# The seven-product scheme starts one chunk earlier in the two SwiGLU up projections behind an RMS norm

## The chip, the core and the metric

The kernel runs on one core of a Trainium2 chip. The metric is device time in microseconds (us), the median of several executions. Five engines share the work: PE (TensorE) multiplies, DVE (VectorE) and ACT (ScalarE) do elementwise work, SP (SyncE) issues the big loads, and POOL (GpSimd) a few small ones. Each engine runs its own instructions in order and waits on semaphores that others raise.

## The reference, cut to what matters

Two blocks run one after the other on 256 tokens of width 1024. The change lies in the first block, which has two layers; each layer has a SwiGLU in front of its mixer and another behind it:

```python
for l in range(DEPTH):                                   # DEPTH = 2
    mod = (cs @ ada_w[l] + ada_b[l]).reshape(...)
    h = _rmsnorm(x, norm_g[l, 0]) * (1.0 + mod[:, 0, 1]) + mod[:, 0, 0]
    x = x + 0.5 * mod[:, 0, 2] * _swiglu(h, ffn_w_gate[l, 0], ffn_w_up[l, 0], ffn_w_down[l, 0])
    ...                                                  # norm, mixer, norm
    x = x + 0.5 * mod[:, 2, 2] * _swiglu(h, ffn_w_gate[l, 1], ffn_w_up[l, 1], ffn_w_down[l, 1])

def _swiglu(h, w_gate, w_up, w_down):
    return (jax.nn.silu(h @ w_gate) * (h @ w_up)) @ w_down   # 1024 -> 2816 -> 1024
```

All of it is float32.

## The kernel before

Tokens are the moving side: `h` is held as 8 tiles of 128 features x 256 tokens. Weights stream from DRAM through `ring`, a buffer of three slots; SP starts a load as soon as the slot's last user is done (`chunk_done`). An up projection (stage `up0` in front of the mixer, `up2` behind it) is 11 chunks of 2 MB, each with 4 groups of 128 outputs (two gate tiles, two up tiles). Between them lie chunks of the modulation weights ("ada"), which DVE multiplies and sums with `ada_sums` (four instructions of line 1792). The string `order` sets the sequence: six ada chunks in `up0`, four in `up2`. Both stages run in both layers, so four times in all.

A chunk goes one of three ways:

- **Chunk 0, the head** (line 778). PE multiplies the not yet normalised `raw`. After its first group PE also sums the squares. DVE takes the reciprocal root (2053), takes out that group (`raw_out`, 1812 and 1813), writes the eight normalised tiles of `h` (`normalise`, line 2071), and ACT adds the shift to each (1493) and raises `h`. Then DVE takes out the other three groups; 1844 joins an up tile with its gate tile when ACT has done the silu.
- **A plain chunk** (line 791). 32 products of 128x128 weights with 256 tokens. PE runs a float32 product as two instructions, so that is 64 in the profile.
- **A chunk with seven products** (`fast_chunk`, line 710): the Strassen-Winograd scheme on 2x2 blocks. It has 7 products of 8 matmuls on 128 tokens, 112 instructions. I call them P1 to P7. DVE must first make sums of the weights (`weight_sums`, lines 1871 to 1876, four instructions of 1024 columns) and, once a stage, of the tokens (`token_sums`, lines 1883 to 1888). P2 needs the first token sum. ACT copies partial results out (`parts_out`), and DVE adds them up (`quadrants`, from line 1909), multiplies gate and up (`gate_up`, 1922) and makes sums for the down projection (`mid_sums`).

A seven-product chunk uses three banks of PSUM in turn: `TRIOS = ((0, 1, 2), (3, 4, 5), (6, 7, 2))`, counted from the first such chunk (`lin.fast`). P1, P3, P5 and P7 use the first bank of a trio, P2 and P6 the second, P4 the third. Bank 2 stands in two neighbouring trios, since 6, 7, 2 is followed by 0, 1, 2. It comes free with the first instruction of `quadrants`, which DVE runs after the weight sums of the next chunk.

Before the change `lin.fast` is 2: chunk 0 is the head, chunk 1 is plain, chunks 2 to 10 use seven products.

Of the kernel before, what the change touches and what calls it, by code (L numbers as in the profile page):

```python
# [15 lines left out]
P = 128  # L16
# [3 lines left out]
DT = D // P  # L20
# [164 lines left out]
def stages():  # L185


    up_rms = lambda src, order: Linear(11, 4, 32 * P, src, order.count("a"), 1, order, 2, biased=2,
                                       token_sums=4, silu=9, mid=9, mid_sums=10)
    down = lambda src: Linear(4, 2, 44 * P, src)  # L190
    down_fast = lambda src: Linear(4, 2, 44 * P, src, fast=0, x_tile=DT)
    norm = with_(uses(b5=1), raw=DT, squares=DT, most_squares=1, root=1, scaled=DT, h=DT)
    ln = with_(uses(b5=1, b6=1), mean=DT, squares=DT, root=1, h=DT)
    ln_fused = with_(ln, most_x=1, scaled=DT)
    logits = with_(uses(b4=2, b5=2, b6=2, b7=2), probs=HG, bias_in=16)
    mix = uses(b0=2, b1=2, b2=2, b3=2)
    prologue = {
        "load_x": with_(uses(b0=1, b1=1, b2=1, b3=1), cond_in=16, cond_set=1, x_tile=DT),
        "bias_rows": uses(b4=1),
        "ada0": Linear(0, 4, 32 * P, "none", adas=4),  # L200
    }
    layer = {
        "norm0": norm, "up0": up_rms("up", "mmmamamamamamamm" "m"), "down0": down_fast("down"),
        "norm1": norm,
        "qk": Linear(6, 4, 32 * P, "w_qk", 6, 1, biased=4), "v": Linear(3, 4, 32 * P, "w_v"),
        "logits0": logits,
        "ccch": Linear(4, 4, 32 * P, "w_ccch"),
        "logits1": logits,
        "cb": Linear(2, 4, 32 * P, "w_cb"),
        "logits2": with_(logits, maxima=1),  # L210
        "gate_a": Linear(2, 4, 32 * P, "w_gates", 2), "mix0": mix,
        "gate_b": Linear(2, 4, 32 * P, "w_gates", gate_c=1), "mix1": mix,
        "weigh": with_(uses(b4=1), weighted=1), "mix2": with_(mix, **uses(b6=1, b7=1)),
        "conv_out": Linear(2, 4, 32 * P, "w_conv_out"),
        "combine": with_(uses(b4=1, b5=1), shares=2, mixed=MIX),
        "attn_out": Linear(1, 8, 32 * P, "w_attn_out", merged=DT),
        "wo": Linear(2, 4, 32 * P, "w_o"), "cond": {"cond_in": 16, "cond_set": 1},
        "norm2": norm, "up2": up_rms("up", "mmmamammammammm"), "down2": down_fast("down"),
    }
    second = {  # L220
        "final_norm": with_(norm, scaled=0, h=0),
        "mod3": {"h": DT},
        "xm": Linear(4, 4, 32 * P, "m_xm", 4, 1, biased=4), "z": Linear(4, 4, 32 * P, "m_z", 2, order="mmamma"),
        "mconv": {"conv": MT, "xc": 1},
        "q": Linear(1, 16, 16 * P, "m_q"), "k": Linear(1, 16, 16 * P, "m_k"),
        "vT": Linear(1, 16, 16 * P, "m_v"),
        "gates": with_(uses(b4=1), gate_rows=1, gate_size=1, gate_logs=1, rows=1),
        "vtok": Linear(1, 8, 16 * P, "m_v_again"),
        "rows_t": with_(uses(b4=1, b5=1, b6=1), floor=1, decays=1),
        "scores": uses(b0=1, b1=1, b2=1, b3=1),  # L230
        "numer": with_(uses(b0=2, b1=2, b2=2, b3=2, b7=1), mvar=MH, mroot=MH, mscale=MH),
        "h_t": with_(uses(b4=2, b5=2, b6=2, b7=2), mh=MT),
        "m_out": Linear(4, 2, 32 * P, "m_out", 3, order="mamamam"), "ln0": ln_fused,
        "up3": Linear(11, 4, 32 * P, "up_3", 11, order="ma" * 11, fast=1, token_sums=4, silu=10, mid=10), "down3": down("down_3"),
        "s5_b": {"s5_dt": 1, "s5_turns": 1, "s5_trig": 1, "s5_lags": 1, "s5_consts": 1, "s5_tables": 1, "s5_waves": 1},
        "ln1": with_(ln, most_x=1),
        "s5_v": Made(3),
        "s5_k": uses(b4=1, b7=1),
        "s5": with_(uses(b0=2, b4=1, b5=1, b6=1, b7=1), free2=2, us_act=11, us_dve=21, states=4, gelu=4, gelu_raw=1, gelu_moved=1),
        "glu": Linear(4, 4, 32 * P, "glu"), "ln2": with_(ln_fused, x_last=1),  # L240
        "router": with_(uses(b4=3, b5=1), top=1, ratio=1, gate=1, picked=1),
        "tokens": uses(b0=1, b1=1, b2=1, b3=1),
    }
    expert = {
        "gather": with_(uses(b4=2, b5=2, b6=2, b7=3), picked=1),
        "upE": Rounds(4, (4, 4, 3), DT, "up_e"), "downE": Sides((0, 8, 15, 22), "down_e"),
        "scatter": uses(b4=2, b5=2, b6=2, b7=2),
    }
    epilogue = {"ln3": with_(ln, scaled=DT), "store": uses(b0=1, b1=1, b2=1, b3=1)}
    return [(prologue, 1), (layer, DEPTH), (second, 1), (expert, NE), (epilogue, 1)]  # L250
# [131 lines left out]
def build(nc, dram, out, periods):  # L382
    plan = Plan()
    with ExitStack() as ctx:
# [9 lines left out]
        h = sb("h_t", [P, DT, S])  # L394
# [32 lines left out]
        mid, act2 = tiles(0, FT), tiles(FT, 2)  # L427
# [52 lines left out]
        def two_columns(a, pairs):  # L480
# [78 lines left out]
        signal = {k: sem(k.replace(" ", "_")) for k in sorted(plan.total)  # L559
                  if k != "chunk" and not k.startswith("of ")}  # L560
        bank_free = [signal[f"free{b}"] for b in range(BANKS)]
# [25 lines left out]
        def reads(p, b, k=0, i=0, per=0):  # L587


            return p.of(f"free{b}", k + 1, i, per)  # L590
# [98 lines left out]
        def _(pe):  # L689
# [154 lines left out]
                    idle_products(p, 13)  # L844

            def ffn(up, down, area, ready=None, after=None, rms_of=None):
                linear(up, lambda k, n: h[:, k, :], ready, rms_of=rms_of,
                       fast=(area, lambda k, t: lambda i: h[:, 4 * k + i, half_of_tokens[t]],
                             lambda k: (signal["token_sums"], up.of("token_sums", k))))
                pe.wait_ge(signal["mid"], up.of("mid", up.what.fasts))  # L850

                linear(down, lambda k, n: mid[:, k, :], after=after,
                       fast=(downs, lambda k, t: lambda i: mid[:, 2 * i + k, half_of_tokens[t]],
                             lambda k: (signal["mid_sums"], up.of("mid_sums", up.what.also["mid_sums"]))))
# [75 lines left out]
            p = place("load_x")  # L930
# [10 lines left out]
            p = place("bias_rows")  # L941
# [34 lines left out]
            p = place("gates")  # L976
# [4 lines left out]
            for pair in range(3 * MT // 2):  # L981
# [3 lines left out]
                for part in range(2):  # L985
                    k = 2 * pair + part
                    src = (mq, mk, mvt)[k // MT][:, k % MT, :]
# [7 lines left out]
            p = place("vtok")  # L995
# [778 lines left out]
        def _(dve):  # L1774
# [140 lines left out]
            def gated_fast(p, buf, dst, np, area, sums=None, normalise=None, down=None):  # L1915

                lin = p.what

                def gate_up(j):
                    n, both = j - lin.fast, area.both(j % 2)  # L1920
                    dve.wait_ge(signal["silu"], p.of("silu", n + 1))
                    dve.tensor_tensor(dst[:, 2 * j:2 * j + 2, :], both[:, 0], both[:, 1], ALU.mult).then_inc(signal["mid"], 1)  # L1922
                    if down:
                        dve.wait_ge(signal["mid"], p.of("mid", n + 1))
                        mid_sums(j)

                done = {n: p.slot(pos) for pos, (kind, n) in enumerate(lin.order) if kind == "main"}
                for pos, (kind, j) in enumerate(lin.order):
                    where = p.slot(pos)
                    if kind == "ada":  # L1930
                        sums(j, 0, where)
                    elif j < lin.fast - 1:
                        gated_chunk(p, buf, dst, j, 0, where, normalise)
                    elif j == lin.fast - 1:
                        token_sums(p, np, area)
                    else:
                        weight_sums(p, j, where, area, done[j - 2] if j > lin.fast + 1 else None)
                        if j == lin.fast:
                            gated_chunk(p, buf, dst, j - 1, 0, done[j - 1])
                            if down:  # L1940
                                dve.wait_ge(bank_free[3], reads(p, 3, lin.at[j - 1][3][2]) + 1)
                                mid_sums(0, lin.fast)
                        else:
                            if j > lin.fast + 1:
                                gate_up(j - 2)
                            quadrants(p, j - 1, area)
                last = lin.chunks - 1
                if down:
                    weight_sums(down, 0, down.slot(0), downs, done[last - 1])
                gate_up(last - 1)  # L1950
                quadrants(p, last, area)
                gate_up(last)
# [714 lines left out]
            p = sp5  # L2667
# [397 lines left out]
```

## Time and profile before

| | us |
|---|---|
| median of 3 runs (3187.36 to 3188.55) | 3187.43 |
| the profiled execution | 3183.68 |
| its span, first to last instruction | 3181.5 |
| PE busy | 3024.8 (95%) |
| DVE busy | 1431.4 (45%) |
| ACT busy | 562.6 (18%) |

Busy time says how full an engine is over the whole program. Which of them holds the end is read from the chain of waits that ended last, and inside a stage from the timeline, where each row gives the start, the duration, and in brackets how long the engine sat idle just before and what it waited for. The four up stages lie at 46 to 191 us, 634 to 775, 851 to 995 and 1440 to 1581. The mean granted clock of TensorE is 0.987 of full speed.

### The profile page before, as it was taken

The page shows a single profiled execution, that of the slowest core. Times are in us where ns is not written, and L with a number is a line of the kernel's source. Part 1 is how long each engine was busy: PE and PEld are TensorE (multiplying, and loading weights), DVE is VectorE, ACT ScalarE, POOL GpSimd, SP SyncE. Part 2 cuts the span into 40 slices and gives each one's busy share as a digit, 9 for nine tenths or more (in the row PEclk, how much of TensorE's full clock was granted, in tenths as well). Part 3 has the DMA queues.
Part 4 walks back from the last instruction along what each step waited for, and adds up shares of the span by engine and source line. Part 5 has one row for each costly group of instructions (what it writes and reads, how often), then busy time and mean ns, then how long its engine had stood idle before and what let it go on. Part 6 is the DMA issues. An engine that isn't in the chain of part 4 may idle for free.

```text
span 3181.5 us, 64710 instructions
## 1 busy us (share of the span) xinstructions
PE 3024.8 (95%) x27390; PEld 2635.5 (83%) x27391; DVE 1431.4 (45%) x2829; ACT 562.6 (18%) x1326; POOL 15.6 (0%) x27
## 2 busy tenths in 40 slices
PE   5999999999999999999999999996999999999999
PEld 4998888899999888889998778985787678767875
DVE  6863333277486423336755448898321112111212
ACT  1111004121111100312111302135211101110111
POOL 0000000000000000000000000000000000000000
PEclk8999999999999999999999999998999999999999
DMA  7746645355375564535637346822287898889885
GB/s 304 309 181 224 239 159 192 129 209 229 138 291 204 200 259 159 192 133 212 242 134 277 133 160 265 322 116 81 102 322 284 307 357 330 317 312 359 321 310 205
DMA packets 55527, 732.94 MB, mean 230 GB/s; under 512 B 6609, under 2 KB 6793, under 8 KB 10805
## 3 DMA queue, kind: packets, MB, share of 16 engines
q1 hardware_dynamic: 51364, 716.68, 58.7%
q0 software_dynamic: 3984, 13.74, 1.2%
q8 instruction: 129, 2.11, 0.3%
q14 instruction: 50, 0.40, 0.0%
HBM read 729.31 MB, written 4.23 MB: 231 GB/s over the span
## 4 chain that ended last, share of the span: by engine, by line
PE 79%; DMA 12%; DVE 6%; issue 2%; ACT 1%; SPq 0%; DVEq 0%; ACTq 0%
PE psum L791 25%; PE psum L710 22%; PE psum L1265 11%; PE psum L1308 10%; DMA ring<-in_up_dram 4%; PE psum L778 3%; DMA ring<-in_up_e_dram 3%; PE psum L865 3%; DVE ring L1792 2%; DMA ring<-in_w_qk_dram 1%; DMA ring<-in_down_e_dram 1%; PE psum L1289 1%; PE psum L1324 1%; DVE work L1778 1%; DMA ring<-in_ada_dram 1%
## 5 line engine op out<-in xcount | busy, mean ns | idle before, releaser
L791 PE MATMUL psum<-h_t,ring 128*128 128x256 f32 x2944 | 642.8, 380 | 8.2 <-DMA ring<-in_w_qk_dram 5.2
L791 PEld LDWEIGHTS psum<-h_t,ring 128*128 128x128 f32 x2944 | 558.0, 190 | 90.5 <-issue 11.5
L1265 PE MATMUL psum<-h_t,ring 128*64 128x96 f32 x11264 | 470.3, 246 | 10.0 <-DMA ring<-in_up_e_dram 9.7
L1265 PEld LDWEIGHTS psum<-h_t,ring 128*64 128x64 f32 x11264 | 466.5, 137 | 13.0 <-issue 11.9
L710 PE MATMUL psum<-work,ring 128*128 128x128 f32 x2880 | 344.5, 276 | 8.6 <-DVE work L1922 8.6
L710 PEld LDWEIGHTS psum<-work,ring 128*128 128x128 f32 x2880 | 333.5, 193 | 9.3 <-issue 9.3
L1308 PE MATMUL psum<-ring,work 128*96 128x512 f32 x704 | 304.1, 593 | 1.2 <-DMA ring<-in_down_e_dram 1.0
L1792 DVE SCALAR_TENSOR_TENSOR ring<-ring,cond 128x1024 f32<-128x1024 f32 x240 | 279.3, 1220 | 57.3 <-DMA ring<-in_ada_dram 57.3
L710 PE MATMUL psum<-work 128*128 128x128 f32 x2528 | 296.7, 276 | 4.2 <-DVE work L1876 4.2
L791 PE MATMUL psum<-work,ring 128*128 128x256 f32 x1344 | 294.9, 382 | 4.2 <-DVE work L1922 2.6
L710 PEld LDWEIGHTS psum<-work 128*128 128x128 f32 x2528 | 290.2, 193 | 4.3 <-DVE work L1876 4.3
L791 PEld LDWEIGHTS psum<-work,ring 128*128 128x128 f32 x1344 | 256.5, 191 | 41.2 <-DVE work L1922 2.7
L1308 PEld LDWEIGHTS psum<-ring,work 128*96 128x96 f32 x704 | 114.1, 163 | 185.5 <-issue 183.1
L2829 DVE TENSOR_TENSOR work<-work,psum 128x256 f32 x176 | 74.1, 421 | 401.1 <-PE psum L1265 401.1
L710 PE MATMUL psum<-h_t,ring 128*128 128x128 f32 x1472 | 181.6, 277 | 14.0 <-DMA ring<-in_up_dram 10.3
L710 PEld LDWEIGHTS psum<-h_t,ring 128*128 128x128 f32 x1472 | 172.0, 192 | 18.3 <-issue 8.6
L2835 DVE COPY work<-psum 128x512 f32<-128x512 f32 x16 | 11.1, 691 | 283.6 <-PE psum L1308 283.6
L778 PE MATMUL psum<-work,ring 128*128 128x257 f32 x448 | 101.8, 385 | 30.2 <-DVE work L2042 26.5
L778 PEld LDWEIGHTS psum<-work,ring 128*128 128x128 f32 x448 | 85.7, 192 | 44.3 <-issue 31.6
L1763 ACT ACTIVATE work<-psum 128x512 f32<-128x512 f32 x16 | 9.6, 597 | 541.7 <-PE psum L1308 541.7
L1871 DVE TENSOR_TENSOR work<-ring 128x1024 f32<-128x1024 f32 (+1 forms) x62 | 82.2, 1326 | 49.6 <-DMA ring<-in_up_dram 49.4
L710 PE MATMUL psum<-h_t,work 128*128 128x128 f32 x736 | 89.7, 275 | 0.0
(375 smaller groups left out, 2449.6 us busy)
## 6 DMA issues: line engine op xcount, KB each, us to landing
ring<-in_up_e_dram SPq DMA_DIRECT2D x64, 2048.0 KB, 7.8
ring<-in_ada_dram SPq DMA_DIRECT2D x60, 2048.0 KB, 7.9
ring<-in_up_dram SPq DMA_DIRECT2D x55, 2048.0 KB, 12.0
ring<-in_down_e_dram SPq DMA_DIRECT2D x32, 1792.0 KB, 8.6
ring<-in_down_dram SPq DMA_DIRECT2D x20, 2816.0 KB, 10.0
ring<-in_up_e_dram SPq DMA_DIRECT2D x32, 1536.0 KB, 8.5
ring<-in_down_e_dram SPq DMA_DIRECT2D x16, 2048.0 KB, 8.3
ring<-in_w_qk_dram SPq DMA_DIRECT2D x12, 2048.0 KB, 9.7
```

The costliest lines, as they stand in the source:

```text
L710: mm = pe.matmul(bank(bank_of)[:, pair * P:(pair + 1) * P], w, right(i), start=(first and pair == 0 and i == 0), stop=(pair == lin.pairs - ...
L778: mm = pe.matmul(psum[:, b * 512:b * 512 + S + 1], ring[:, slot, (m * DT + k) * P:(m * DT + k + 1) * P], raw[:, k, :], start=(k == 0), sto ...
L791: mm = pe.matmul(half(b), w, moving(k, j * lin.groups + m), start=(k == 0), stop=(k == depth - 1))
L865: mm = pe.matmul(half(b), h[:, k, t * P:(t + 1) * P], ring[:, slot, k * 512 + n * S:k * 512 + (n + 1) * S], start=(k == 0), stop=(k == DT ...
L1265: mm = pe.matmul(half(b)[lo:hi, 0:width], w[:, lo:hi], h[:, k, 0:width], start=(k == 0), stop=(k == lin.depth - 1))
L1289: mm = pe.matmul(half(b)[:, 0:width], h_tok[:, t, f * P:(f + 1) * P], sel[:, t, 0:width], start=(t == 0), stop=(t == TT - 1))
L1308: mm = pe.matmul(bank(2 * side + n)[0:slots(n), :], mid[:, k, n * P:n * P + slots(n)], ring[:, slot, (k - first) * 512:(k - first + 1) * 512],
L1324: mm = pe.matmul(half(b), y_pos[0:slots(n), n, f * P:(f + 1) * P], gate_sel[0:slots(n), n, :], start=(n == 0), stop=(n == lists - 1))
L1778: dve.tensor_tensor(o, a, b, op).then_inc(dve_done, steps.one())
L1792: e = dve.scalar_tensor_tensor(w, w, 1.0, cond[:, :], ALU.mult, ALU.mult, accum_out=col)
L1871: dve.tensor_tensor(s1, a21, a22, ALU.add).then_inc(signal["weight_sums"], 1)
L2829: dve.tensor_tensor(o, o, half(b), ALU.mult).then_inc(bank_free[b], 1)
```

## The change

`fast` becomes 1, so chunk 1 uses seven products too, and the trios are counted from it: chunk 4 now has banks 0, 1, 2, where it had 6, 7, 2. PE waits for all of `h` in front of chunk 1. On DVE the order around the head changes.

```diff
-    up_rms = lambda src, order: Linear(11, 4, 32 * P, src, order.count("a"), 1, order, 2, biased=2,
-                                       token_sums=4, silu=9, mid=9, mid_sums=10)
+    up_rms = lambda src, order: Linear(11, 4, 32 * P, src, order.count("a"), 1, order, 1, biased=2,
+                                       token_sums=4, silu=10, mid=10, mid_sums=11)
...
+                all_h = lambda: pe.wait_ge(signal["h"], ready.of("h", DT)) if up.what.head else None
...
+                    elif j == 0 and lin.head:
+                        def normalise_first():
+                            normalise()
+                            weight_sums(p, 1, done[1], area)
+
+                        gated_chunk(p, buf, dst, 0, 0, where, normalise_first)
+                        token_sums(p, np, area)
+                        if down:
+                            dve.wait_ge(bank_free[3], reads(p, 3, lin.at[0][3][2]) + 1)
+                            mid_sums(0, 1)
...
-                        weight_sums(p, j, where, area, done[j - 2] if j > lin.fast + 1 else None)
+                        if j > 1 or not lin.head:
+                            weight_sums(p, j, where, area, done[j - 2] if j > lin.fast + 1 else None)
+                        if j == lin.fast and lin.head:
+                            continue
```

On DVE, at the head of `up0`, the rows before run from the normalised tiles straight to the head's second, third and fourth group:

```order
L2071 SCALAR_TENSOR_TENSOR h_t<-x_t,gain,rms 128x256 x8
L1811 ISA
L1812 COPY small<-psum 128x1 [waits full1]
L1813 TENSOR_TENSOR work<-psum,rms 128x256
L1842 REGISTER_ALU
L1843 ISA [waits dve_done]
L1844 SCALAR_TENSOR_TENSOR work<-work,small 128x256 [waits biased]
L1812 COPY small<-psum 128x1 [waits full2]
```

At the same place of the changed kernel, whose lines are numbered up to 14 higher there:

```order
L2085 SCALAR_TENSOR_TENSOR h_t<-x_t,gain,rms 128x256 x8
L1871 ISA
L1872 TENSOR_TENSOR work<-ring 128x1024 [waits chunk_in2]
L1873 TENSOR_TENSOR ring<-ring 128x2x512
L1874 ISA
L1875 TENSOR_TENSOR work<-work,ring 128x1024 [waits weight_sums]
L1876 REGISTER_ALU
L1877 TENSOR_TENSOR work<-ring,work 128x1024 [waits weight_sums]
L1812 ISA
L1813 COPY small<-psum 128x1 [waits full1]
L1814 TENSOR_TENSOR work<-psum,rms 128x256
```

The four weight sums of chunk 1 (`ring` is the weight buffer, `work` holds the sums) now stand between the normalised tiles and the second group of the head; the token sums still come behind the head's fourth group.

On PE, chunk 1 of `up0` before:

```order
L773 REGISTER_ALU [waits chunk_in2]
L791 MATMUL psum<-h_t,ring 128x256 [waits h,free0]
L791 MATMUL psum<-h_t,ring 128x256 [waits h] x7
L791 MATMUL psum<-h_t,ring 128x256 [waits free1]
L791 MATMUL psum<-h_t,ring 128x256 x7
```

On PE, chunk 1 of `up0` now:

```order
L730 REGISTER_ALU [waits chunk_in2]
L710 MATMUL psum<-h_t,ring 128x128 [waits h,free0]
L710 MATMUL psum<-h_t,ring 128x128 x7
L727 ISA
L738 ISA [waits free1,weight_sums]
L710 MATMUL psum<-work 128x128 [waits token_sums]
L710 MATMUL psum<-work 128x128 x7
```

The second product, on the sums in `work`, waits for bank 1, which the head's second group frees on DVE, and for the first token sum.

On PE, chunk 4 of `up0` before:

```order
L730 ISA [waits chunk_in1]
L710 MATMUL psum<-h_t,ring 128x128 [waits free6]
L710 MATMUL psum<-h_t,ring 128x128 x7
L727 REGISTER_ALU
L710 MATMUL psum<-work 128x128 [waits free7,weight_sums]
```

On PE, chunk 4 of `up0` now:

```order
L730 REGISTER_ALU [waits chunk_in1]
L710 MATMUL psum<-h_t,ring 128x128 [waits free0]
L710 MATMUL psum<-h_t,ring 128x128 x7
L727 REGISTER_ALU
L710 MATMUL psum<-work 128x128 [waits free1,weight_sums]
```

Chunk 4 moved from the trio 6, 7, 2 to 0, 1, 2. Its fourth product uses bank 2 in both kernels; the user of bank 2 before it was chunk 2, and is now chunk 3.

## Rows read from the trace of the kernel before

**Rows 1.** The page: busy time; shares of the chain that ended last.
```profile
PE 3024.8 (95%) x27390; PEld 2635.5 (83%) x27391; DVE 1431.4 (45%) x2829; ACT 562.6 (18%) x1326; POOL 15.6 (0%) x27
PE 79%; DMA 12%; DVE 6%; issue 2%; ACT 1%; SPq 0%; DVEq 0%; ACTq 0%
```

**Rows 2.** The chain in order of time, first `up0`: start, us, what.
```profile
56.90 13.81 PE psum L791 x64
70.71 12.52 PE psum L710 x112
```

**Rows 3.** Timeline, head of the first `up0`: start, us, engine, line, operation.
```profile
52.86 0.15 DVE L1812 COPY small<-psum 128x1 f32<-128x1 f32 x1
...
56.74 13.97 PE L791 MATMUL psum<-h_t,ring 128*128 128x256 f32 x64
...
60.48 1.22 DVE L1871 TENSOR_TENSOR work<-ring 128x1024 f32<-128x1024 f32 x1
...
65.15 0.41 DVE L1852 TENSOR_TENSOR work<-work,psum 128x256 f32<-128x256 f32 x1
```

**Rows 4.** Timeline, head of the second `up0`.
```profile
858.32 0.15 DVE L1812 COPY small<-psum 128x1 f32<-128x1 f32 x1
...
860.83 0.48 DVE L1844 SCALAR_TENSOR_TENSOR work<-work,small 128x256 f32<-128x256 f32 x1 [2.03 <-ACT work L1451]
...
861.11 13.97 PE L791 MATMUL psum<-h_t,ring 128*128 128x256 f32 x64
861.23 0.15 DVE L1812 COPY small<-psum 128x1 f32<-128x1 f32 x1
...
861.63 0.15 DVE L1812 COPY small<-psum 128x1 f32<-128x1 f32 x1
...
862.29 0.49 DVE L1844 SCALAR_TENSOR_TENSOR work<-work,small 128x256 f32<-128x256 f32 x1 [0.18 <-ACT work L1451]
862.69 0.68 DVE L1883 TENSOR_TENSOR work<-h_t 128x512 f32<-128x512 f32 x1
```

**Rows 5.** Timeline, head of the second `up2`.
```profile
1446.73 0.15 DVE L1812 COPY small<-psum 128x1 f32<-128x1 f32 x1
...
1450.61 13.97 PE L791 MATMUL psum<-h_t,ring 128*128 128x256 f32 x64
```

**Rows 6.** Timeline, chunk 4 of the second `up2`, with the issue of its load.
```profile
1477.98 12.12 SPq L643 DMA_DIRECT2D ring<-in_up_dram  x2
...
1490.70 1.22 DVE L1871 TENSOR_TENSOR work<-ring 128x1024 f32<-128x1024 f32 x1 [0.92 <-DMA ring<-in_up_dram]
...
1490.80 2.05 PE L710 MATMUL psum<-h_t,ring 128*128 128x128 f32 x16 [1.20 <-DMA ring<-in_up_dram]
...
1496.25 1.95 PE L710 MATMUL psum<-h_t,ring 128*128 128x128 f32 x16
...
1497.03 0.41 DVE L1909 TENSOR_TENSOR work<-work,psum 128x256 f32<-128x256 f32 x1
```

**Rows 7.** Timeline, first `up0`: waits of PE in chunks 5 and 8.
```profile
115.23 0.41 DVE L1909 TENSOR_TENSOR work<-work,psum 128x256 f32<-128x256 f32 x1
...
115.70 2.05 PE L710 MATMUL psum<-h_t,ring 128*128 128x128 f32 x16 [0.56 <-DVE work L1909]
...
156.06 2.05 PE L710 MATMUL psum<-h_t,ring 128*128 128x128 f32 x16 [1.08 <-DVE work L1909]
```

**Rows 8.** Timeline of PE: first matmuls behind longer idle times, in four stages.
```profile
190.64 2.72 PE L710 MATMUL psum<-work,ring 128*128 128x128 f32 x22 [2.15 <-DVE work L1922]
...
995.18 4.35 PE L710 MATMUL psum<-work,ring 128*128 128x128 f32 x22 [2.15 <-DVE work L1922]
...
1938.34 5.26 PE L710 MATMUL psum<-work 128*128 128x128 f32 x32 [4.18 <-DVE work L1876]
...
2072.11 28.11 PE L791 MATMUL psum<-work,ring 128*128 128x256 f32 x129 [2.55 <-DVE work L1922]
```

**Rows 9.** Busy time by stretch: stretch, length, PE, PEld, DVE, ACT, POOL, then PEclk.
```profile
996.50:998.00 1.50, 1.50 (x9) 1.50 (x9) 1.41 (x5) 0.00 (x0) 0.00 (x0) 0.50 0.91 390
```

## What the change should do to the time

> **What bounds the kernel now.** I read the page first: PE is busy for 95% of the span, and 79% of the chain that ended last is PE [rows 1]. Time that PE gains or loses inside an up stage therefore reaches the end, unless a load or DVE holds PE up at the next step anyway. So I followed the chain through the stages, and then read the timeline of each up stage row by row: the head, chunk 1, and each later place where PE sat idle. The four up stages repeat each other almost to the hundredth; where one row stands for several stages I say for how many.
>
> Two things are to be seen. A plain chunk costs PE 13.81 us and a seven-product chunk 12.52 us, so 1.79 us for each of the seven products [rows 2]. And chunk 1 is the place where DVE has the most to do in a row, while chunk 4 is where PE waits for a load in all four stages (1.20 to 1.35 us).
>
> **Part 1, the products.** Chunk 1 falls from 13.81 to 12.52 us on PE [rows 2]: -1.29 us, four times, -5.2 us. This is on the path, since PE goes on without a gap from the head to chunk 1 and on to chunk 2.
>
> **Part 2, a new wait for the token sum.** P1 of chunk 1 needs only `h`, which is complete before the head ends. P2 needs the first token sum and bank 1, and DVE now reaches both late, because it does the weight sums first. Step by step for the first `up0`, counted from the start of the second group's copy, at 52.86 us, when DVE is done with normalising [rows 3]:
> - The four weight sums take 65.15 - 60.48 = 4.67 us [rows 3]. Chunk 1 landed long before, so they don't wait.
> - The second group, from its copy to the third group's copy: from copy to join 862.29 - 861.63 = 0.66, and from join to the next step 861.23 - 860.83 = 0.40, together 1.06 us; ACT's silu has long been done by then.
> - From the third group's copy to the token sums: 862.69 - 861.23 = 1.46 us [rows 4].
> - The first token sum 0.68 us [rows 4], and 0.06 us until PE sees it (in rows 7, DVE's instruction of 0.41 us started at 115.23, and PE at 115.70).
>
> The sum is 7.93 us, so the token sum is there at 60.79. The head leaves PE free at 56.74 [rows 3], and P2 could start after P1, at 58.53. The wait is 2.26 us. A product behind a wait shows 2.05 instead of 1.95 us [rows 6], so 0.10 more: 2.36 us. Both `up2` have the same offset: in the second one 1450.61 - 1446.73 = 3.88 us [rows 5] against 56.74 - 52.86 = 3.88, and in the first 3.89. In the second `up0` DVE normalises later: the offset is 861.11 - 858.32 = 2.79 us [rows 4], and the wait grows to 7.93 - 2.79 - 1.79 = 3.35, with the restart 3.45 us. Together 3 x 2.36 + 3.45 = +10.5 us.
>
> So chunk 1 gets longer: by 1.07 us three times and by 2.16 us once. The later products don't wait: P3 needs the third token sum signal, 1.2 us after the first, while P2 takes 1.79 us. The weight sums of chunk 2 follow on DVE at about 64 us, before PE needs them. Weight sums no longer run during chunk 2's first steps, and `quadrants`, `gate_up` and `mid_sums` of chunk 1 come in; DVE waits there for loads anyway, so I cost them at nothing. Without that cover they would cost up to 2 us a stage.
>
> **Part 3, the banks.** Chunk 4 now follows chunk 3 on bank 2. In the second `up2` chunk 4 lands at 1490.7: DVE starts its weight sums and PE its P1 together. DVE reaches the first instruction of `quadrants` (chunk 3) at 1497.03 and ends it at 1497.44, while P4 of chunk 4 started at 1496.25 [rows 6]. In the changed kernel P4 must wait for that instruction: 1.19 + 0.06 + 0.10 = 1.35 us. The first `up2` has the same rows with 1.18. Both together: +2.7 us. The load doesn't come earlier to help, as it is issued when PE ends chunk 2 (1477.98) [rows 6], and PE ends that later. Chunks 7 and 10 meet the same pair of banks, but in `up2` DVE is there in time (its step at 1530.41, P4 at 1533.77).
>
> In both `up0` such waits exist already, in chunks 5 and 8, with 0.56 and 1.08 us [rows 7]; they go, and chunks 4 and 7 get them, up to 1.35 each. There an ada chunk stands beside every chunk, and loads set the pace between waits (0.48 us in chunk 6) [rows 7]: two chunks later a wait in the one comes off the load wait of the other or adds to it. Following the loads through, the new waits put chunk 8 behind by 1.4 us, and chunk 8's own old wait makes up for it. I take 0 for both stages; the bounds are -1.8 us each (old waits gone, new ones hidden) and +1.1 each (both new ones at 1.35, against 1.64 gone).
>
> **Part 4, the clock.** After an idle time of PE the granted clock can be at the lower of its two levels, 1.2 instead of 2.4 GHz. Of four waits of 2.15 us at the hand-over to the down projection, one was followed by slow matmuls: 4.35 us for the same 22 instructions that took 2.72 elsewhere [rows 8], at a granted clock of 0.50 [rows 9]. That cost 1.63 us. A wait of 2.55 us left the clock alone, one of 4.18 us didn't: 32 matmuls took 5.26 us [rows 8], where 32 take 3.74 at full clock. The new waits are 2.3 us (three) and 3.4 us (one). By these rows the short ones fall rarely and the long one lies between 2.55 and 4.18; I take one fall, +1.6 us, and 0 to 4 as bounds (0 to +6.5 us).
>
> The Trainium skill, "TensorE: Matmul & The Clock Gate", Part 1, says that the monitor which sets the clock runs freely and doesn't start with the kernel, so that the same kernel shows other numbers of slow matmuls from run to run. The trace agrees in that four equal waits of 2.15 us had one fall. By that rule the number of falls is a matter of position, and the sum has no fixed last term.
>
> **The sum.** -5.2 + 10.5 + 2.7 + 0 + 1.6 = +9.6 us. Against the profiled execution of 3183.68 us that is 3193.3; that execution was 3.75 us below the median of the runs shown, so the median goes from 3187.43 to **3197.0 us**. 0.2% of this kernel is 6.4 us, about what a measurement can tell from no change.
>
> **The rivals.**
> - **Most new waits meet the lower clock** (three or four falls). For it: the waits stand one behind each norm, where nothing else keeps PE busy, and all are longer than the 2.15 us that fell once. Against it: one of four, and 2.55 without. Three falls give 8.0 + 4.9 = 12.9, four 14.5 us: 3200.3 to 3202.
> - **The loads swallow the late chunk 1** (not slower). PE waits 1.2 to 1.35 us for the load of chunk 4 in all four stages, so a chunk 1 that is 1.07 us late would cost nothing if that load kept its time. Part 2 would then be worth only 2.16 - 1.3 = 0.9, and the whole 0.9 + 2.7 = +3.6 us: 3191.0, within the bound. It decides wherever the load of chunk 4 is issued by something other than PE's end of chunk 2. Against it: the load is issued within 1 us of that end [rows 6].
> - **The token sums come in time** (faster, but within the bound): if DVE reached them before P1 ends, part 2 would be 0 and the clock untouched, -5.2 + 2.7 = -2.5 us: 3184.9. It decides if the offset of 2.8 to 3.9 us were 6 or more. Against it: rows 3 to 5.
> - **No wait for bank 2** in `up2`, and the old ones in `up0` gone: -5.2 + 10.5 - 3.6 = +1.7 us, 3189.1.
>
> That the change doesn't do what it says can be left out: the order on PE and DVE shows it.
>
> **How the numbers follow.** My forecast with 0 to 2 falls has a chance of 0.72 (3195.4 to 3198.7 by the terms, 3193 to 3201 with the bounds of part 3); three or four falls 0.12; loads swallow it 0.06; no wait for bank 2 0.05; token sums in time 0.05. The range leaves out the not-slower rivals and the top of the first one: 3193.0 to 3201.0. Slower by over 0.2% (above 3193.8): the forecast less a small part at its lower end, and the first rival: 0.83. Within: the other three and that part, 0.14. Faster by over 0.2% would need the token sums in time and the bank waits gone: 0.03.
>
> **What would show it.** In each up stage of the changed kernel, PE should sit idle in chunk 1 before P2 for 2.2 to 2.3 us (3.3 in the second `up0`), released by DVE's first token sum, and in chunk 4 before P4 for about 1.25 us, released by `quadrants`. Chunk 1 should take 14.9 us (16.0). The matmuls behind the chunk 1 wait tell the falls: 16 instructions take 1.95 at full clock. I am wrong if P2 waits under 1.3 us, if chunk 4's load wait is gone, or if the old waits of `up0` stay.

## The result, and the profile after

| | before | after |
|---|---|---|
| median, us | 3187.43 | 3201.11 |
| the profiled execution, us | 3183.68 | 3202.76 |
| its span, us | 3181.5 | 3200.7 |
| mean granted clock | 0.987 | 0.983 |

The changed kernel is slower: 13.7 us by the medians, a ratio of 1.0041 with an interval of 1.0027 to 1.0056. Timed again beside other runs of before it was 1.0045 (1.0030 to 1.0061). All medians below are of the fast executions; one slow execution each of the last two kernels (3850 and 10672 us) is left out.

The page after, busy time and the shares of the chain that ended last, against [rows 1]. PE has 192 instructions more (four chunks of 112 for four of 64), and DVE holds 8% of the chain instead of 6%:

```profile
PE 3033.6 (95%) x27582; PEld 2648.4 (83%) x27583; DVE 1456.0 (45%) x2869; ACT 569.5 (18%) x1342; POOL 15.6 (0%) x27
PE 77%; DMA 11%; DVE 8%; issue 3%; ACT 1%; SPq 0%; DVEq 0%; ACTq 0%
```

Where it went shows in the busy time by stretch. Each row runs from the head's second group to the start of the down projection, one row for each up stage in order; the columns are those of [rows 9], and the third number from the end is the clock. Before:

```profile
46.30:190.64 144.34, 138.38 (x1122) 134.24 (x1120) 112.00 (x187) 28.82 (x68) 0.00 (x0) 1.00 0.68 267
634.48:775.17 140.69, 137.23 (x1122) 133.86 (x1120) 102.54 (x171) 28.81 (x68) 0.00 (x0) 1.00 0.60 232
850.67:995.18 144.51, 138.28 (x1121) 134.15 (x1120) 111.99 (x188) 28.84 (x68) 0.00 (x0) 1.00 0.64 247
1440.17:1580.76 140.59, 137.24 (x1122) 133.86 (x1120) 102.54 (x171) 28.82 (x68) 0.00 (x0) 1.00 0.60 231
```

After:

```profile
46.52:196.05 149.53, 140.24 (x1169) 137.76 (x1168) 118.03 (x197) 30.41 (x72) 0.00 (x0) 0.98 0.66 257
641.80:785.08 143.28, 136.43 (x1170) 134.35 (x1168) 108.51 (x181) 30.42 (x72) 0.00 (x0) 1.00 0.59 227
860.32:1009.69 149.37, 139.10 (x1170) 136.28 (x1168) 118.27 (x198) 30.42 (x72) 0.00 (x0) 0.99 0.62 241
1455.06:1599.98 144.92, 138.05 (x1169) 135.97 (x1168) 108.50 (x181) 30.41 (x72) 0.00 (x0) 0.99 0.58 224
```

The four stages are longer by 5.19, 2.59, 4.86 and 4.33 us, 17.0 together. The second shows the clock at 1.00; in the fourth it is 0.99, in the third 0.99 and in the first 0.98.

The timeline of PE in chunk 1 after. P1 and P2 of the first `up0`, then P2 of the other three stages:

```profile
56.97 1.95 PE L710 MATMUL psum<-h_t,ring 128*128 128x128 f32 x16
60.97 5.47 PE L710 MATMUL psum<-work 128*128 128x128 f32 x32 [2.06 <-DVE work L1884]
...
656.32 3.81 PE L710 MATMUL psum<-work 128*128 128x128 f32 x32 [2.13 <-DVE work L1884]
...
876.28 5.46 PE L710 MATMUL psum<-work 128*128 128x128 f32 x32 [3.58 <-DVE work L1884]
...
1469.58 5.44 PE L710 MATMUL psum<-work 128*128 128x128 f32 x32 [2.14 <-DVE work L1884]
```

P2 waits for DVE's first token sum (line 1884) in all four stages. The 32 matmuls of P2 and P3 then take 3.81 us once and 5.44 to 5.47 us three times. The granted clock of the first of these stretches is 0.68, so part of it ran at the lower level of 1.2 GHz; that of the second is 1.00 (stretch, length, PE busy, clock):

```profile
60.97:66.24 5.27, 5.27 (x32) 0.68 0.57 243
...
656.32:660.00 3.68, 3.68 (x33) 1.00 0.82 347
```

DVE around it in the first `up0`, which answers to [rows 3]: the first weight sum, the second group's copy, the fourth group's join, the first token sum:

```profile
53.09 1.22 DVE L1872 TENSOR_TENSOR work<-ring 128x1024 f32<-128x1024 f32 x1
...
57.76 0.15 DVE L1813 COPY small<-psum 128x1 f32<-128x1 f32 x1
...
59.83 0.49 DVE L1845 SCALAR_TENSOR_TENSOR work<-work,small 128x256 f32<-128x256 f32 x1 [0.18 <-ACT work L1452]
60.23 0.68 DVE L1884 TENSOR_TENSOR work<-h_t 128x512 f32<-128x512 f32 x1
```

From 53.09 to PE's start at 60.97 it is 7.88 us (the prediction's sum was 7.93).

Chunk 4, P4 behind bank 2, in the first `up0` and the second `up2`, which answers to [rows 6], and a load wait of chunk 6 in the first `up0`:

```profile
106.03 2.05 PE L710 MATMUL psum<-h_t,ring 128*128 128x128 f32 x16 [1.24 <-DVE work L1910]
...
127.89 2.54 PE L710 MATMUL psum<-h_t,ring 128*128 128x128 f32 x16 [1.94 <-DMA ring<-in_up_dram]
130.22 4.91 PE L710 MATMUL psum<-work 128*128 128x128 f32 x32
...
1515.38 2.05 PE L710 MATMUL psum<-h_t,ring 128*128 128x128 f32 x16 [1.08 <-DVE work L1910]
```

And the hand-over to the down projection, which answers to [rows 8]. Before, one of four was slow; after, three of four:

```profile
196.05 3.73 PE L710 MATMUL psum<-work,ring 128*128 128x128 f32 x22 [2.15 <-DVE work L1923]
...
785.08 2.72 PE L710 MATMUL psum<-work,ring 128*128 128x128 f32 x22 [2.15 <-DVE work L1923]
...
1009.69 4.35 PE L710 MATMUL psum<-work,ring 128*128 128x128 f32 x22 [2.15 <-DVE work L1923]
...
1599.98 4.34 PE L710 MATMUL psum<-work,ring 128*128 128x128 f32 x22 [2.15 <-DVE work L1923]
```

### The profile page after: what moved, and what is told of

Its sections match the earlier page's. It is cut to its first block, busy times and chain, and to the rows that moved or that the text cites. A ratio compares the mean times of both kernels' runs of the same rounds, so it can differ in the third digit from the quotient of the medians.

```text
span 3200.7 us, 65252 instructions
## 1 busy us (share of the span) xinstructions
PE 3033.6 (95%) x27582; PEld 2648.4 (83%) x27583; DVE 1456.0 (45%) x2869; ACT 569.5 (18%) x1342; POOL 15.6 (0%) x27
## 4 chain that ended last, share of the span: by engine, by line
PE 77%; DMA 11%; DVE 8%; issue 3%; ACT 1%; SPq 0%; DVEq 0%; ACTq 0%
PE psum L791 24%; PE psum L710 23%; PE psum L1266 11%; PE psum L1309 9%; DMA ring<-in_up_dram 4%; DMA ring<-in_up_e_dram 4%; PE psum L866 3%; PE psum L778 2%; DVE ring L1793 2%; DMA ring<-in_w_qk_dram 1%; PE psum L1290 1%; PE psum L1325 1%; DVE work L1779 1%; DMA ring<-in_w_v_dram 1%; DMA ring<-in_ada_dram 1%
## 5 line engine op out<-in xcount | busy, mean ns | idle before, releaser
L791 PE MATMUL psum<-h_t,ring 128*128 128x256 f32 x2688 | 587.1, 380 | 7.9 <-DMA ring<-in_w_qk_dram 4.9
L791 PEld LDWEIGHTS psum<-h_t,ring 128*128 128x128 f32 x2688 | 509.2, 190 | 84.0 <-issue 11.3
L710 PE MATMUL psum<-work,ring 128*128 128x128 f32 x3008 | 362.8, 277 | 8.6 <-DVE work L1923 8.6
L710 PEld LDWEIGHTS psum<-work,ring 128*128 128x128 f32 x3008 | 351.0, 194 | 9.4 <-issue 9.4
L710 PE MATMUL psum<-work 128*128 128x128 f32 x2656 | 318.9, 280 | 14.1 <-DVE work L1884 9.9
L710 PEld LDWEIGHTS psum<-work 128*128 128x128 f32 x2656 | 311.8, 196 | 15.0 <-DVE work L1884 6.0
L791 PEld LDWEIGHTS psum<-work,ring 128*128 128x128 f32 x1344 | 257.5, 192 | 40.2 <-DVE work L1923 2.2
L710 PE MATMUL psum<-h_t,ring 128*128 128x128 f32 x1600 | 197.7, 277 | 18.5 <-DMA ring<-in_up_dram 12.3
L710 PEld LDWEIGHTS psum<-h_t,ring 128*128 128x128 f32 x1600 | 187.3, 192 | 22.9 <-issue 10.6
L778 PEld LDWEIGHTS psum<-work,ring 128*128 128x128 f32 x448 | 85.7, 192 | 44.1 <-issue 31.4
L710 PE MATMUL psum<-h_t,work 128*128 128x128 f32 x800 | 97.5, 275 | 0.0
```

The lines of the kernel that those rows point to most:

```text
L710: mm = pe.matmul(bank(bank_of)[:, pair * P:(pair + 1) * P], w, right(i), start=(first and pair == 0 and i == 0), stop=(pair == lin.pairs - ...
L778: mm = pe.matmul(psum[:, b * 512:b * 512 + S + 1], ring[:, slot, (m * DT + k) * P:(m * DT + k + 1) * P], raw[:, k, :], start=(k == 0), sto ...
L791: mm = pe.matmul(half(b), w, moving(k, j * lin.groups + m), start=(k == 0), stop=(k == depth - 1))
```

## The experiments

A "fall" below means matmuls behind a wait that run at the lower clock for some us. Its price is mostly 1.6 to 1.7 us: 5.44 to 5.47 instead of 3.81, 4.34 instead of 2.72. "Filled" means that PE runs products in a wait whose results nobody reads. "Stage lengths" are the lengths of the stretches shown above, from the head's second group to the start of the down projection. The diffs are shortened ("...") and the comments in them are mine.

### The changed kernel again

No edit. It is there so that the next three can be set against it on the same chip.

> The changed kernel again, beside the others. Its profiled execution had 16 slow instructions or more (lower granted clock) behind three of the four new waits in chunk 1, each worth about 1.6 us. If these falls are a matter of position, a new execution shows another number of them (0 to 4 in chunk 1), while the waits themselves stay at 2.1 us (three) and 3.6 us (one), and chunk 1 takes 14.9 us where no fall is and 16.5 where one is. If the falls belong to the waits as such, the same three or four are there again. Median against before: +10 to +15 us by both.

Measured: 3203.19 against 3190.00 of before, +13.2 us. The waits are in the same places (2.06, 2.14, 3.10 and 2.14 us before P2), but the falls are not: P2 is slow in the first three stages and not in the last, and of the hand-overs the first two are slow. Two rows of it that were the other way round above, P2 in the first and in the second `up2`:

```profile
655.72 5.44 PE L710 MATMUL psum<-work 128*128 128x128 f32 x32 [2.14 <-DVE work L1884]
...
1470.71 3.81 PE L710 MATMUL psum<-work 128*128 128x128 f32 x32 [2.14 <-DVE work L1884]
```

So the places of the waits belong to the kernel, and the falls to the execution. (The wait of the second `up0` was 3.10 us here and 3.58 above; the other three agree within 0.01.)

### The trios turned: no wait for bank 2 in chunk 4

```diff
-                for b, many in zip(TRIOS[(j - fast) % len(TRIOS)], (3, 2, 1)):
+                for b, many in zip(TRIOS[(j - fast + turn) % len(TRIOS)], (3, 2, 1)):   # turn = 2
```

> Only the turn of the bank trios differs from the changed kernel: the first seven-product chunk takes 6, 7, 2, so that chunks 5 and 8 meet the doubled bank 2 as before the change, and no longer chunk 4. My theory of the banks: the wait of 1.1 to 1.2 us before the fourth product of chunk 4 is gone in all four stages; in both up2 nothing takes its place (-1.35 us each), in both up0 the waits of chunks 5 and 8 come back (0 in sum). The wait before the second product of chunk 1 stays at 2.1 and 3.6 us, since the token sums come as late as before. The time falls by 2.7 us against the changed kernel. Rival, that P2 waits for bank 1 and not for the token sum: with bank 7 in place of bank 1 the wait would fall under 1 us in all four stages, and the time by 6 us or more.

Measured: 3202.53, +12.5 us. P4 of chunk 4 waits in no stage any more. In this trace neither `up2` has a fall inside the stage, and they last

```profile
640.07:782.21 142.14, 136.16 (x1170) 134.28 (x1168) 108.49 (x181) 30.42 (x72) 0.00 (x0) 1.00 0.60 229
...
1452.99:1594.84 141.85, 136.16 (x1170) 134.28 (x1168) 108.47 (x181) 30.42 (x72) 0.00 (x0) 1.00 0.60 229
```

142.14 us where the changed kernel without a fall had 143.28: 1.14 us, the size of the bank wait. In both `up0` the waits of chunks 5 and 8 are back. P2 of chunk 1 waits as before (2.06, 2.14, 3.17, 2.13), so bank 1 is not what it waits for: it is the token sum. The bank term is real in the trace, and too small to show in the median: 2.7 us less than the changed kernel was expected, and 0.7 less was measured.

### Trios turned, and the token sums right behind the weight sums

```diff
+                            token_sums(p, np, area)        # behind weight_sums(p, 1, ...)
...
                         gated_chunk(p, buf, dst, 0, 0, where, normalise_first)
-                        token_sums(p, np, area)
```

> As the kernel with turned trios, and the four token sums stand right behind the weight sums of chunk 1, ahead of the head's second, third and fourth group. If the token sums alone held PE up, PE goes through chunk 1 without a wait in three stages (chunk 1 12.5 us, and 0.8 us more in the second up0), and the time falls by 9 to 11 us against the kernel with turned trios. My theory, that DVE's work behind the norm is too long whatever its order: the second product is in time, but ACT's first copy for chunk 1 now stands behind its silu of the head's third group, which DVE takes out 2.6 us later than now, so the third product waits for that copy: 2.4 us in three stages and 2.6 us behind a wait of 0.8 in the second up0. Time then within 2 us of the kernel with turned trios.

Measured: 3204.93, no gain. P2 now starts without a wait in three stages, and P3 waits instead. In the second `up0` both wait, P2 for 2.25 us (0.8 was expected) and P3 for 1.47. P2 and P3 of the first `up0`:

```profile
58.88 1.95 PE L710 MATMUL psum<-work 128*128 128x128 f32 x16
62.87 2.46 PE L710 MATMUL psum<-work 128*128 128x128 f32 x16 [2.04 <-ACT work L1381]
```

The releaser is ACT's copy of P1 and P2 (line 1381). On ACT it stands behind the second silu of the head, and that waited 6.17 us for DVE to take out the third head group (line 1814), which the token sums have pushed back:

```profile
61.86 0.51 ACT L1452 ACTIVATE work<-work,small 128x256 f32<-128x256 f32 x1 [6.17 <-DVE work L1814]
62.27 0.36 ACT L1381 ACTIVATE work<-psum 128x256 f32<-128x256 f32 x1
```

So moving the token sums alone only moves the 2 us from P2 to P3. That DVE's work is too long "whatever its order", as I expected, does not follow: the interleaved order below does away with the wait.

### The wait before P2 filled with products that nobody reads

```diff
+                if n == 0 and lin.head:
+                    for _ in range(9):                     # between P1 and P2
+                        pe.matmul(bank(7)[:, 0:P], ones[:, :], ones[:, :], start=True, stop=True)
```

> The changed kernel, with nine products of ones by ones (18 instructions, 2.0 us) into the idle bank 7 on PE between the first and the second product of chunk 1; their results are never read. The wait for the token sum is thus filled, but not shortened. If the lower clock behind it comes from PE's idle time, chunk 1 takes 14.9 us in three stages and 16.0 in the second up0, with the second product at full clock, and the time falls by 1.6 us for each fall that the changed kernel has there (three in its profile: 4 to 5 us). If the clock falls for another reason, slow instructions stay in chunk 1 or at its start, and the time stays within 1 us of the changed kernel. If the products get in the way (bank 7, weight loads), chunk 1 gets longer.

Measured: 3195.49, +5.5 us against before (interval of the ratio 1.0005 to 1.0024) and 7.7 us less than the changed kernel on the same chip. Nothing that the kernel needs comes earlier; PE only stays busy. P2 is fast in all four stages, in the second `up0` too, where 1.19 us of the wait are left. The first `up0`, then the second:

```profile
60.97 2.17 PE L737 MATMUL psum<-ones 128*128 128x128 f32 x18
63.20 3.84 PE L710 MATMUL psum<-work 128*128 128x128 f32 x32
...
876.39 3.84 PE L710 MATMUL psum<-work 128*128 128x128 f32 x32 [1.19 <-DVE work L1887]
```

So it is PE's idling that brings the falls in chunk 1. One trace could be chance, but the mean granted clock over all executions agrees: 0.984 for the changed kernel (9), 0.987 with the wait filled (11), 0.987 for before (24). The gain is larger than I can count: eight of the twelve P2 waits in three traces of unfilled kernels were followed by a fall, 2.7 a run, or 4.4 us.

### Seven products in chunk 1 with DVE's order interleaved

On DVE the head now runs: first weight sum, first token sum, two weight sums, head groups two and three, two token sums, fourth weight sum, fourth token sum, head group four. The trios are turned.

```diff
...                                                        # turn = 2 as above
+                            first[0](); tokens[0](); first[1](); first[2]()   # weight sums, token sums
...
+                        def behind(m):                     # behind head group m, counted from 0
+                            if m == 2:
+                                tokens[1](); tokens[2](); first[3](); tokens[3]()
...
-                        token_sums(p, np, area)
```

> The seven products in chunk 1 stay, the trios are turned so that the first such chunk takes banks 6, 7, 2, and DVE's order at the head is interleaved: first weight sum, first token sum, second and third weight sum, head groups two and three, two token sums, fourth weight sum, fourth token sum, head group four. If the 10.5 us of waits are owed to the order on DVE alone (theory), chunk 1 shows no wait in three stages and about 0.65 us in the second up0; then each stage from the start of its head to the start of its down projection is shorter than in the kernel before by 0.8 to 1.3 us (0.6 in the second up0), no clock falls in chunk 1, and the median lies 3 to 5 us below the kernel before (ratio 0.9985 to 0.999). If the loads or ACT's copies give the wait back (rival: as P3 did when only the token sums were moved), a wait of 1.5 to 2 us shows at P3 or later in chunk 1 and the median is 4 to 10 us above the kernel before.

Measured: 3187.54 against 3188.52, ratio 1.0000 (0.9989 to 1.0011). That is between the two expectations. Chunk 1 is as the theory has it: P1 to P3 of the first `up0` without a gap, and the only wait left, before P3 of the second `up0`:

```profile
56.89 1.95 PE L710 MATMUL psum<-h_t,ring 128*128 128x128 f32 x16
58.67 3.74 PE L710 MATMUL psum<-work 128*128 128x128 f32 x32
...
865.86 2.05 PE L710 MATMUL psum<-work 128*128 128x128 f32 x16 [0.53 <-DVE work L1919]
```

The stages tell where the gain went:

```profile
46.45:190.80 144.35, 136.97 (x1170) 134.50 (x1168) 117.62 (x197) 30.42 (x72) 0.00 (x0) 1.00 0.69 267
636.39:775.90 139.51, 135.93 (x1170) 134.20 (x1168) 108.18 (x181) 30.41 (x72) 0.00 (x0) 1.00 0.61 234
851.15:996.20 145.05, 137.40 (x1169) 134.65 (x1168) 117.88 (x198) 30.37 (x72) 0.00 (x0) 1.00 0.64 248
1440.62:1579.83 139.21, 135.93 (x1170) 134.21 (x1168) 108.19 (x181) 30.41 (x72) 0.00 (x0) 1.00 0.61 234
```

Both `up2` are shorter than before by 1.18 and 1.38 us, the 1.29 us of part 1. The first `up0` is as long as before (144.35 and 144.34) and the second longer by 0.54, though PE is busy for 1.41 and 0.88 us less: with an ada chunk beside every chunk, PE waits longer for later loads. The longest load wait of before behind chunk 4 of the first `up0`, in chunk 6, and that of this kernel, in chunk 7:

```profile
123.59 2.05 PE L710 MATMUL psum<-h_t,ring 128*128 128x128 f32 x16 [0.48 <-DMA ring<-in_up_dram]
```

```profile
137.14 2.05 PE L710 MATMUL psum<-h_t,ring 128*128 128x128 f32 x16 [1.39 <-DMA ring<-in_up_dram]
```

Chunk 5 too waits for its load, 1.31 us, where it did not before. So in these traces seven products in chunk 1 pay in `up2` alone, 2.6 us together.

### The same, and the hand-overs filled

```diff
+                if up.what.head:                           # ahead of the wait for mid
+                    b, _, k = up.what.at[up.what.chunks - 2][1]
+                    pe.wait_ge(bank_free[b], reads(up, b, k) + 1)
+                    for _ in range(9):
+                        pe.matmul(bank(b)[:, 0:P], ones[:, :], ones[:, :], start=True, stop=True)
```

> As the kernel with the interleaved order, and PE runs nine products of ones by ones (18 instructions, about 2.2 us) in the wait of 2.15 us in front of each of the four first down projections; their result is never read. If PE's idle time is what lowers the granted clock (theory), the first 22 instructions of all four down projections take 2.7 us and the median falls by another 2 to 5 us (one to three falls of 1.6 us), 5 to 9 us below the kernel before. If the clock falls by its own pace whatever PE does there (rival), the median is that of the interleaved order within 1 us and slow matmuls show elsewhere.

Measured: 3182.02 against 3188.52, ratio 0.9979 (0.9969 to 0.9988), the fastest of all kernels here. All four down projections start at full clock. The fill in the first `up0` and the 22 instructions behind it:

```profile
188.61 2.17 PE L855 MATMUL psum<-ones 128*128 128x128 f32 x18
190.93 2.72 PE L710 MATMUL psum<-work,ring 128*128 128x128 f32 x22
```

The traces account for about as much: the stage lengths add up to 567.36 us against 570.13 before, -2.8, and 17 of the 28 unfilled hand-overs in seven traces were slow, 2.4 a run, 3.9 us. Together 6.7, and 6.5 were measured. The falls as the cause are argued here from that count. The mean granted clock doesn't show them: it is 0.987 over the twelve executions of the interleaved kernel and 0.987 over these twelve. And this trace has a fall that none of the other nine has, at the head of the second `up0`, where the same 16 matmuls took 3.72 us before, behind a wait of 2.04:

```profile
845.76 5.40 PE L778 MATMUL psum<-work,ring 128*128 128x257 f32 x16 [2.03 <-issue]
```

### The kernel before with its hand-overs filled

The same lines in the kernel before.

> The kernel before, with the same nine products of ones by ones in the wait in front of each first down projection. Theory: no fall at these four places, median 2 to 5 us below the kernel before. Rival (the clock falls by its own pace): within 1 us of the kernel before.

Measured: 3186.52 against 3188.52, ratio 0.9996 (0.9987 to 1.0005). This doesn't decide: 3.9 us less lies inside the interval, none as well. No hand-over is slow in its trace, but two load waits of chunk 4 that were 1.30 and 1.35 us before are 2.27 and 2.03 here, and both are followed by a fall. The first:

```profile
687.00 2.62 PE L710 MATMUL psum<-h_t,ring 128*128 128x128 f32 x16 [2.27 <-DMA ring<-in_up_dram]
689.41 4.84 PE L710 MATMUL psum<-work 128*128 128x128 f32 x32
```

Why these loads came later was not tried.

### The changed kernel with both fills

The nine products between P1 and P2, and the nine at the hand-over.

> The changed kernel with both fills: nine products of ones by ones between P1 and P2 of chunk 1 and nine in front of each first down projection. Set against the kernel before with the second fill alone it shows what the change costs when the clock has no place to fall: by terms 1 to 3 of the prediction 8.0 us (theory). If the change costs more than these terms by something other than the clock (rival), the difference is 10 us or more.

Measured: 3193.96; 7.4 us above the kernel before with its hand-overs filled, near the 8.0 of the theory. Its trace has no fall in any up stage or hand-over, so it shows parts 1 to 3 of the prediction by themselves:

```profile
46.60:192.76 146.16, 141.26 (x1206) 138.60 (x1204) 118.14 (x198) 30.39 (x72) 0.00 (x0) 1.00 0.67 262
636.67:779.75 143.08, 140.45 (x1205) 138.37 (x1204) 108.43 (x181) 30.40 (x72) 0.00 (x0) 1.00 0.59 228
855.03:1002.09 147.06, 141.31 (x1206) 138.64 (x1204) 118.21 (x198) 30.38 (x72) 0.00 (x0) 1.00 0.63 244
1445.60:1588.72 143.12, 140.44 (x1205) 138.37 (x1204) 108.45 (x181) 30.37 (x72) 0.00 (x0) 1.00 0.59 228
```

Against the stages of before, which have no fall inside either, that is +1.82, +2.39, +2.55 and +2.53: 9.3 us. (The stages of the kernel before with filled hand-overs are no measure for it, as they hold the two falls at loads.) Against the kernel before without a fill the median is 5.4 us higher, and 9.3 less the 3.9 of the hand-overs is 5.4 too. But the kernel with P2's wait alone filled was 5.5 above the runs of before beside it, so between these two kernels the second fill shows no gain.

## Why the prediction was right, and which term was too small

The direction was right, and so were the mechanisms. The median came out 4.1 us above the forecast and 0.1 us above the end of the range. (The range's lower end was tighter than its own terms: 3195.4 less twice the bound of 1.8 in part 3 is 3191.8, not 3193.)

- **Part 1** holds on PE: without waits chunk 1 is shorter by what was said, as the two `up2` of the interleaved kernel show (-1.18 and -1.38 us for -1.29).
- **Part 2** was right to about 0.2 us. Forecast: 2.26 us before P2 in three stages, 3.35 in the second `up0`. Measured: 2.06 to 2.14, and 3.58 (3.10 and 3.17 in other executions). The 7.93 us on DVE were 7.88. Chunk 1 without a fall took 14.87 us (652.24 to 667.11) for the 14.9 forecast. The order of DVE's instructions makes this wait: with the token sums moved ahead as a block it only shifts to P3, with the interleaved order it is gone but for 0.53 us in one stage.
- **Part 3** was right in `up2`: 1.08 us plus the restart in both, 1.14 by the turned trios, for 1.35. In `up0` I took 0. The kernel with both fills gives it: +1.82 and +2.55 where parts 1 and 2 make 1.07 and 2.16, so +0.75 and +0.39, inside the bound of 1.1. How much of that is waits for bank 2 and how much load waits that took back a gain, as in the interleaved kernel, the runs don't separate. The rival that the loads swallow the late chunk 1 held in part there: chunk 4's load wait fell to 0.57 and 0.48 us, from 1.29 and 1.35 before, while in `up2` it grew to 1.48 and 1.50. The prediction's 0.48 us of chunk 6 has no row in group 7; it is the row at 123.59 shown above.
- **Part 4 is the step that failed.** I took one fall for four new waits, from one slow hand-over in four [rows 8]. Four rows of one execution were too few: over seven traces it is 17 of 28 hand-overs, and 8 of 12 waits before P2. At that share the new waits cost 4 x 8/12 x 1.65 = 4.4 us instead of 1.6. The rival with three or four falls, 3200.3 to 3202, is what the changed kernel's profile shows in chunk 1: three. It had been given a chance of 0.12.

Put together: 9.3 us for parts 1 to 3 and 4.4 for the falls are 13.7; 13.7 and 13.2 were measured. That it agrees so closely is in part luck, since the interval of the first ratio runs from 8.6 to 17.9 us. The two profiles differ by more, 19.1 us. That is 9.3, the three falls in chunk 1 (5.0), two more slow hand-overs than before (3.3) and a fall at a load wait in chunk 6 (1.7), together 19.3. Stage by stage it is less close: without the hand-overs these terms give 16.0 for the four stages, and 17.0 were shown above.

The sentence of the Trainium skill that I cited ("TensorE: Matmul & The Clock Gate", Part 1: the number of slow matmuls differs from run to run) is borne out by the two executions of the changed kernel, whose waits agree in three of four stages and whose falls don't. I cited it and still took the count of one execution for the share.

What stays open: the kernel with P2's wait filled was only 5.5 us above before, with at most 7.7 by its interval, where 9.3 would be left by the trace. That leaves some 2 to 4 us which no trace accounts for. Executions of before may have falls at load waits that its one trace lacks, as the kernel with filled hand-overs had; this wasn't tried.

## What to carry to other kernels

Before a stage on PE is shortened, add up what the engine that feeds it has to do between the last common event and the first operand: here 7.9 us of DVE against 5.7 of PE made a faster chunk slower, and an interleaved order of the same instructions removed nearly all of the wait. Give every new idle time of PE of about 2 us the price of a fall times its share over several executions, at the same place where that can be had, and never take that share from a few rows of one. Where such a wait can't be removed, products that nobody reads can keep PE's clock up. At P2 of this kernel that was worth 7.7 us by the medians. At the four hand-overs it is 3.9 us by the traces, but the medians show a clear gain in only one of three pairs of kernels (5.5 us; 2.0 and nothing in the others).

## What the runs showed of the hardware that I had not expected

The same wait, to the hundredth of a us (2.14 before P2), is followed by the lower clock in one execution and not in the next. In ten traces, 80 waits of PE of 1.00 to 1.81 us stand in the up stages behind the head; behind 79 of them the matmuls ran at full clock, and the other one (1.47 us) came within 5 us of a wait of 2.25 us. Of the 40 waits of 2.06 to 3.6 us before P2 (in three kernels) and at unfilled hand-overs 25 were followed by a fall, of 1.4 to 1.7 us. So were three of the four waits of 1.89 to 2.25 us in chunk 1 of the kernel with its token sums moved. Of six load waits of 1.89 to 2.27 us five were followed by one too; the sixth, 1.91 us in chunk 6 in the second run of the changed kernel, wasn't. The length of the wait isn't the whole of it: of the ten waits of 1.78 to 2.23 us at the head of the second `up0`, one in each trace, only the one of 2.03 us shown above was followed by a fall. What sets these apart was not tried.
